# The last projection piece in two column halves, and the two transposes of a token tile side by side

## The reference

```
def layer_norm(x, g, b):
    mu = mean(x); var = mean(square(x - mu))
    return (x - mu) * rsqrt(var + LN_EPS) * g + b

x = layer_norm(DEEPNORM_ALPHA * x + h, ln_mix_g[l], ln_mix_b[l])
x = layer_norm(DEEPNORM_ALPHA * x + swiglu(x, w_gate, w_up, w_down), ln_ffn_g[l], ln_ffn_b[l])
```

## Time and profile before

| | us |
|---|---|
| median of 3 runs | 1202.56 (1202.39 to 1202.94) |
| span of the profiled execution, first to last instruction | 1201.0 |
| TensorE busy | 1191.7 |
| VectorE busy | 881.1 |
| ScalarE busy | 661.8 |
| last matmul ends | 1194.2 |
| last VectorE instruction ends | 1199.0 |

### The profile page before, as it was taken

One profiled execution on the slowest core, in us unless ns is written; L12 is line 12 of the kernel. 1 busy time (PEld: TensorE's weight loads), 2 busy tenths in 40 slices (PEclk: granted clock), 3 DMA queues, 4 the chain that ended last, 5 costly groups with the idle time before them and its releaser, 6 DMA issues.

```text
span 1201.0 us, 16544 instructions
## 1 busy us (share of the span) xinstructions
PE 1191.7 (99%) x6611; PEld 1025.8 (85%) x6611; DVE 881.1 (73%) x1227; ACT 661.8 (55%) x871; POOL 52.7 (4%) x75
## 2 busy tenths in 40 slices
PE   9999999999999999999999999999999999999997
PEld 8888888888777888888899888888889977888886
DVE  6977989847786798884688877776467667777744
ACT  6545666634566666663587645444337775544430
POOL 0000000000000000000005200000012001000000
PEclk9999999999999999999999999999999999999999
DMA  9755555564534555556434556555526433755530
GB/s 359 248 206 192 174 179 192 187 221 170 195 114 138 188 180 179 203 201 216 160 102 141 185 211 236 191 195 191 179 91 229 176 140 106 253 202 175 198 119 35
DMA packets 32652, 217.80 MB, mean 181 GB/s; under 512 B 3760, under 2 KB 4032, under 8 KB 8000
## 3 DMA queue, kind: packets, MB, share of 16 engines
q1 hardware_dynamic: 30704, 210.39, 49.5%
q0 software_dynamic: 1728, 6.29, 1.6%
q10 hardware_dynamic: 144, 0.07, 0.0%
HBM read 215.67 MB, written 1.05 MB: 180 GB/s over the span
## 4 chain that ended last, share of the span: by engine, by line
PE 99%; DVE 1%; DMA 0%; ACT 0%; issue 0%
PE ps L963 43%; PE ps L893 24%; PE ps L899 14%; PE ps L901 4%; PE ps L915 2%; PE ps L912 2%; PE ps L911 2%; PE ps L1004 1%; PE ps L977 1%; PE ps L1032 1%; PE ps L1014 1%; PE ps L1096 1%; DMA t<-in_cst 0%; PE ps L1042 0%; PE ps L1081 0%; PE ps L926 0%
## 5 line engine op out<-in xcount | busy, mean ns | idle before, releaser
L963 PE MATMUL ps<-t,t 128*128 128x512 f32 (+3 forms) x2328 | 538.4, 387 | 0.0
L1552 DVE TENSOR_TENSOR t<-t,t 128x2048 fp32r<-128x2048 f32 (+3 forms) x200 | 448.8, 2257 | 101.9 <-PE ps L963 87.7
L963 PEld LDWEIGHTS ps<-t,t 128*128 128x128 f32 x2328 | 423.1, 188 | 81.5 <-issue 1.8
L1205 ACT CAST t<-t 128x2048 fp32r<-128x2048 f32 (+3 forms) x200 | 374.6, 1883 | 202.3 <-PE ps L963 106.0
L893 PE MATMUL ps<-t,t 128*128 128x512 f32 x1274 | 305.8, 390 | 0.0
L893 PEld LDWEIGHTS ps<-t,t 128*128 128x128 f32 x1274 | 238.9, 188 | 51.2
L899 PEld LDWEIGHTS ps<-t,t 128*128 128x128 f32 x1456 | 187.2, 191 | 7.4
L899 PE MATMUL ps<-t,t 128*128 128x256 f32 x1456 | 189.5, 283 | 0.0
L1687 DVE TENSOR_REDUCE t<-ps 128x512 f32<-128x1024 f32 x40 | 49.0, 1225 | 44.3 <-PE ps L901 44.3
L1640 DVE SCALAR_TENSOR_TENSOR t<-t,t,t 128x254 f32<-128x254 f32 (+1 forms) x176 | 73.2, 478 | 10.2 <-ACT t L1230 10.2
L1270 ACT CAST t<-t 128x512 fp32r<-128x512 f32 x44 | 27.3, 620 | 91.2 <-DVE t L1671 91.2
(11 more groups left out here) (220 smaller groups left out, 846.0 us busy)
## 6 DMA issues: line engine op xcount, KB each, us to landing
t<-in_wts SPq DMA_DIRECT2D x192, 1024.0 KB, 4.9
t<-in_rows POOLq DMA_DIRECT2D x12, 512.0 KB, 4.4
t<-in_wts SPq DMA_DIRECT2D x4, 528.0 KB, 4.1
t<-in_wts SPq DMA_DIRECT2D x2, 768.0 KB, 4.8
t<-in_wts SPq DMA_DIRECT2D x2, 592.0 KB, 3.8
t<-in_x_in SPq DMA_DIRECT2D x2, 512.0 KB, 4.3
out<-t SPq DMA_DIRECT2D x4, 256.0 KB, 2.0
t<-in_wts SPq DMA_DIRECT2D x2, 256.0 KB, 6.3
```

The costliest lines, as they stand in the source:

```text
L963: ins = mm(ps[:, t_bank(stage, t, j), 0:c1 - c0], a, w[:, k, c0:c1], start=kt == 0 and part == 0, stop=kt == KTS[stage] - 1 and part == 2)
L1205: copy(wh[:, k, 0:w], wraw[:, r, 0:w]).then_inc(s_hi, 1)
L1552: tt(wl[:, k, 0:w], wraw[:, r, 0:w], wh[:, h, 0:w].bitcast(F32), ALU.subtract).then_inc(s_lo, 1)
```

## The change

At b = 8 the parts of (1,1) become "piece" steps: first all 6 k-tiles for columns 512 to 767, in the bank as before (bank 3), and then all 6 for columns 768 to 1023, in bank 4, where they start a new sum; the earlier k-tiles of these columns stay in bank 3. VectorE's `added_piece` follows each: the first makes ALPHA * x plus bank 3 for all 512 columns and the statistics of the first 256; the second adds bank 4 to the last 256 columns and makes their statistics. Tile 1's statistics are now in four records of 256 columns, tile 0's stay in two of 512.

At the inner norms the two turns of a tile stand side by side. Tile 0: behind the third of the four part steps of (1,1) at norms 1 to 4 (before: second and third), behind the fourth at norms 5 to 7 (before: third and fourth). Tile 1, in the next projection's head: behind two lo steps at norms 1 to 4 (before: none and two), behind six at norms 5 to 7 (before: four and eight).

```
--- end_steps, 5 <= b < 8
-            if n in (2, 3):
-                out.append(("turn", b, 0, n - 2))
+            if n == 3:
+                out += [("turn", b, 0, 0), ("turn", b, 0, 1)]
--- end_steps, other b
+    if b == 8:
+        for piece in range(2):
+            out += [("piece", stage, kt, piece) for kt in kts] + [("add_piece", piece)]
+        return out + [("stats", 8, 1)] + [(kind, 8, 1, j) for kind in ("centre", "norm") for j in range(2)]
-        if b < 8 and n in (1, 2):
-            out.append(("turn", b, 0, n - 1))
+        if b < 8 and n == 2:
+            out += [("turn", b, 0, 0), ("turn", b, 0, 1)]
--- head_steps
-    n = 4 if b >= 5 else 0
-    out = [("hi", stage, kt, 0) for kt in range(8)] + lo[:n] + [("turn", b, 1, 0)]
-    n, m = n, (8 if b >= 5 else 2)
-    out += lo[n:m] + [("turn", b, 1, 1)] + lo[m:]
+    n = 6 if b >= 5 else 2
+    out = [("hi", stage, kt, 0) for kt in range(8)] + lo[:n] + [("turn", b, 1, 0), ("turn", b, 1, 1)] + lo[n:]
--- t_part
+                    at = 0
+                    if piece is not None:
+                        at = 256 * piece
+                        c0, c1 = c0 + at, c0 + at + 256
+                    first, bank = kt == 0, t_bank(stage, t, j)
+                    if piece == 1:
+                        at, bank, first = 0, 4, kt == KTS[stage] - LAST[stage] * per
+                        pe.wait_ge(*ffn_read(3, 20))
+                    ins = mm(ps[:, bank, at:at + c1 - c0], a, w[:, k, c0:c1],
+                             start=first and part == 0, stop=kt == KTS[stage] - 1 and part == 2)
--- VectorE
+        def added_piece(i):
+            dve.wait_ge(s_t, T_AT["piece", "down3", KTS["down3"] - 1, i])
+            cols = slice(512, 1024) if i == 0 else slice(768, 1024)
+            if i == 0:
+                dve.own(stt(out=XN[:, 1, cols], in0=X[:, 1, cols], scalar=ALPHA, in1=acc(1, 1), op0=ALU.mult, op1=ALU.add))
+            else:
+                dve.own(tt(XN[:, 1, cols], XN[:, 1, cols], ps[:, 4, 0:256], ALU.add))
+            dve.settle()
+            dve.own(nc.vector.bn_stats(out=st[:, 44 + 6 * i:50 + 6 * i], in_=XN[:, 1, 512 + 256 * i:768 + 256 * i]))
--- VectorE, added at b = 8, t = 1 (j = 0)
+                    for i in range(2):
+                        dve.own(nc.vector.bn_stats(out=st[:, 32 + 6 * i:38 + 6 * i], in_=rs[:, 256 * i:256 * i + 256]))
--- VectorE, stats at b = 8
+            dve.own(nc.vector.bn_aggr(out=st[:, 16 * t + 12:16 * t + 14], in_=st[:, 32:56] if t else st[:, 0:12]))
```

More of the change, by code:

```diff
@@ L241, in end_steps @@
             out += [("stats", b, 0)] + normed_steps(b, 0, 0) + normed_steps(b, 0, 1)
+    if b == 8:
+        for piece in range(2):
+            out += [("piece", stage, kt, piece) for kt in kts] + [("add_piece", piece)]
+        return out + [("stats", 8, 1)] + [(kind, 8, 1, j) for kind in ("centre", "norm") for j in range(2)]
     for n, kt in enumerate(kts):
         out.append(("part", stage, 1, 1, kt))
-        if b < 8 and n in (1, 2):
-            out.append(("turn", b, 0, n - 1))
+        if b < 8 and n == 2:
+            out += [("turn", b, 0, 0), ("turn", b, 0, 1)]
     out.append(("add", b, 1, 1))
-    if b == 8:
-        return out + [("stats", b, 1)] + [(kind, b, 1, j) for kind in ("centre", "norm") for j in range(2)]
     return out + [("rest", b, 0, 0), ("stats", b, 1), ("rest", b, 0, 1), ("norm", b, 1, 0), ("norm", b, 1, 1)]
@@ L344, in releases @@
         return kt == KTS[stage] - 1 or ((t, j) == (1, 1) and kt % PER[stage] == PER[stage] - 1)
+    if s[0] == "piece":
+        _, stage, kt, piece = s
+        return kt == KTS[stage] - 1
     return False
@@ L940, in second_half, with t_part @@
             ins.then_inc(s_f, 1)
-        def t_part(step, stage, kt, t, js, passes=(0, 1, 2)):
+        def t_part(step, stage, kt, t, js, passes=(0, 1, 2), piece=None):
             per = PER[stage]
@@ L962, in t_part @@
                     c0, c1 = cols[j]
-                    ins = mm(ps[:, t_bank(stage, t, j), 0:c1 - c0], a, w[:, k, c0:c1],
-                             start=kt == 0 and part == 0, stop=kt == KTS[stage] - 1 and part == 2)
+                    at = 0
[8 more added lines that the diff above has]
+                             start=first and part == 0, stop=kt == KTS[stage] - 1 and part == 2)
             if releases(step):
@@ L1160, in pe_program @@
                 t_part(s, k[0], k[3], k[1], [k[2]])
+            elif kind == "piece":
+                t_part(s, k[0], k[1], 1, [1], piece=k[2])
             elif kind == "turn":
@@ L1577, in added @@
                 dve.wait_ge(s_add, 4 * (b - 1) + 2 * t + j + 1)
-                dve.own(nc.vector.bn_stats(out=o, in_=rs))
+                if t == 0:
+                    dve.own(nc.vector.bn_stats(out=o, in_=rs))
+                else:
+                    for i in range(2):
+                        dve.own(nc.vector.bn_stats(out=st[:, 32 + 6 * i:38 + 6 * i], in_=rs[:, 256 * i:256 * i + 256]))
                 return
@@ L1599, in stats @@
             dve.settle()
-            dve.own(nc.vector.bn_aggr(out=st[:, 16 * t + 12:16 * t + 14], in_=st[:, 16 * t:16 * t + 12]))
+            dve.own(nc.vector.bn_aggr(out=st[:, 16 * t + 12:16 * t + 14], in_=st[:, 32:56] if t else st[:, 0:12]))
             dve.settle()
@@ L1925, in dve_program @@
                 mean(*k)
+            elif kind == "add_piece":
+                added_piece(*k)
             elif kind == "stats":
```

## The result

| | before | changed |
|---|---|---|
| median, us | 1202.58 (1202.17 to 1203.29, 21 runs) | 1204.45 (1204.10 to 1204.79, 21 runs) |
| span of the profiled execution, us | 1201.0 | 1203.1 |

The ratio is 1.0015, 95% interval 1.0009 to 1.0021: slower, by 1.87 us between the medians, which is clear of zero and inside the 0.2% that the prediction puts between a difference and none. The forecast was 1204.8.

A forecast was written before the change was run, and what follows sets the result against it. Bound: TensorE's own stream plus what follows its last matmul. Waits at norms 5 to 7 (+2.76), grouping (-0.27) and tail (-0.30) sum to +2.2 us on the 1202.6 median: 1204.8, range 1202.9 to 1205.9.

The forecast's parts named there:

- the gain from grouping: Inner norms: each change between transposes and matmuls costs about 0.02 us; 14 pairs grouped give -0.27 us.
- Norms 5 to 7, tile 0: Next head's first weight load waits for ScalarE's copy of the first turn: 0.55 us per norm, bounds 0.51 to 0.57.
- Norms 5 to 7, tile 1: With only two low passes after both turns, TensorE waits for copy and subtraction: 0.37 us per norm, bounds 0.30 to 0.43.
- Norms 1 to 4: Inner norms 1 to 4: no new wait; head's first weight load is free at 1.34 us, just when due.
- The tail: After the last wide matmuls: TensorE +0.24, VectorE's way to the aggregate -0.55, aggregate +0.01; in all -0.30 us.
- The shorter price of the Trainium skill: Tail matmuls at N divided by 2.4 GHz plus about 2.5 ns: only +0.05 us for TensorE; not used.
- Dear restarts: Norms 5 to 7: nine restarts after waits at 0.11 us each, tile 1 paying 0.43 in full; +3.4 us, 1206.0, chance 0.22.
- Tile 1 covered: Norms 5 to 7: low passes and load overlap hide tile 1's chain, only tile 0 pays; +1.1 us, 1203.7, chance 0.16.
- No stall: Inner norms: the moved turns cause no waits and only the two gains are left; -0.6 us, 1202.0, chance 0.07.
- One step failed: Norm 5, tile 1: VectorE's norm halves end near 710.2 and 710.9, behind copies some 0.1 us later, making no wait.

The follow-up runs named there:

- e3: The kernel before with only tile 0's two turns of norms 5 to 7 moved behind the last group of matmuls; 1204.16 against 1202.48 us, ratio 1.0013.
- e4: The kernel before with only tile 1's two turns of norms 5 to 7 moved behind the sixth low pass; 1203.29 against 1202.48 us, ratio 1.0007.
- e10: The kernel before with tile 0's two turns of norms 1 to 4 behind the last group of matmuls; 1204.54 against 1202.48 us, ratio 1.0016.
- e1: The kernel before with the tail's change alone, all inner-norm turns where they stood; 1202.43 against 1202.48 us, ratio 0.9999.
- e6: The changed kernel with grouped turns of norms 5 to 7 earlier: tile 0 behind the third group, tile 1 behind four low passes; 1203.52 against 1202.47 us.
- e2: The kernel before with the turns grouped at norms 1 to 4 alone; 1202.49 against 1202.48 us, ratio 0.9999.
- e5: The changed kernel with the turns of norms 5 to 7 back where they stood before; 1202.07 against 1202.47 us, ratio 0.9996.

## Why the prediction was right

The mechanism and the places came out, and so did the sum (+2.2 forecast, +1.9 between the medians, +2.0 in the profile's own terms); the waits are a little smaller than I made them. The profile's figures for norms 5 to 7 have the gain from grouping in them, which the forecast had as a term of its own (0.02 us for each tile), so it is added back here.

- **Norms 5 to 7, tile 0** (0.55 taken, 0.51 to 0.57 bounds): 0.49 to 0.53 in e3, which changes nothing else, so 0.51 to 0.55. The load follows the copy by 0.06 us, at the low end of the wake-up times I had (0.05 and 0.12).
- **Norms 5 to 7, tile 1** (0.37 taken, 0.30 to 0.43): 0.29 to 0.31 in e4, which changes nothing else, so 0.31 to 0.33. The load that waits for the subtraction is 0.43 us idle, as computed, and about 0.1 of it comes back. In the changed kernel, with the matmuls' starts read one by one, the third matmul starts at 713.42, right behind its load at 713.41, where in the undisturbed stream a matmul starts a step of 0.23 behind its load; the next one then stands 0.34 behind it and not 0.23. The load that waits 0.21 us for the copy costs little: its matmul (712.76) is a plain step of 0.23 behind the one ahead of it, and the next step is 0.28, so 0.05 us. I took the middle of the bounds, and the low one was nearer.
- **Why tile 0 gets nothing back.** A load that follows transposes stands right ahead of its matmul even without a wait, so its lateness passes on in full. Before, behind the second turn of norm 5:

```profile
705.66 4.43 PEld L963 LDWEIGHTS ps<-t,t 128*128 128x128 f32 x20
705.69 4.83 PE L963 MATMUL ps<-t,t 128*128 128x512 f32 x20
```

- **Norms 1 to 4**: -0.15 us for -0.16, and no wait. The copy frees the head's first load 1.29 us after the first transpose (704.94 to 706.23 in e3) and the load is due at 1.34, so only 0.05 us is to spare. e10 shows the same wait there as soon as the cover is taken away.
- **Grouping itself**: at norms 2 to 4 it is 0.04 us or a little more for each norm, at norm 1 only 0.01. At norms 5 to 7 it isn't separable from the waits.
- **The tail** (-0.30): -0.24. TensorE's part is +0.23 (+0.24 taken) and VectorE's way to the aggregate -0.53 (-0.55 taken); the term most mis-sized is the aggregate, +0.05 for twelve more numbers where I had 0.01. The shorter price of the Trainium skill (page "TensorE: Matmul & The Clock Gate", section "Wait — 56ns, not 53.3ns?") gives as an estimate a last sum 0.05 us later; e1 measured 0.23, and this agrees with the trace's own steps.
- **The sum.** Norms 5 to 7 were forecast at +2.76 less 0.12 for their six pairs, so +2.64, and took +2.42; the tail is 0.06 short the other way. That makes 0.16 of the 0.35 us between the forecast and the median. The rest lies between the profile's own terms (+2.03) and the medians (+1.87, with an interval from 1.1 to 2.5 us) and in the forecast's rounding; no run separates it further.
- **Rivals.** Dear restarts: no. The step behind tile 1's late matmul is 0.11 us longer, the very amount that this rival took, but the matmul itself starts earlier behind its load by more than that, and behind tile 0's wait the first step is 0.31 us, as in the undisturbed stream behind transposes. Tile 1 covered: no, e4. No stall: no, e3.
- **One step failed, without weight in the sum.** I had the norm halves of tile 1 at norm 5 end some 0.1 us later than before, because the statistics stand behind the copies on ScalarE. They come earlier, at 709.12 against 709.35, which is 0.32 us along the stream. What I had left out is that VectorE's chain starts with the last group of (1,1), and that group now ends 0.45 us earlier. The copies do hold the chain up, but by 0.12 us only. L1597 (L1624 after) adds the epsilon and needs ScalarE's sum of squares; it stands behind VectorE's centring (L1629, L1656 after). Before:

```profile
706.63 1.54 DVE L1629 SCALAR_TENSOR_TENSOR t<-t,t,t 128x512 f32<-128x512 f32 x2
707.57 0.19 ACT L1221 ACTIVATION_READ_ACCUMULATOR ps<-t,t 128x1 f32 x1
708.09 0.15 DVE L1597 TENSOR_SCALAR t<-t 128x1 f32<-128x1 f32 x1
```

After:

```profile
706.28 1.54 DVE L1656 SCALAR_TENSOR_TENSOR t<-t,t,t 128x512 f32<-128x512 f32 x2
...
707.62 0.20 ACT L1234 ACTIVATION_READ_ACCUMULATOR ps<-t,t 128x1 f32 x1
707.86 0.15 DVE L1624 TENSOR_SCALAR t<-t 128x1 f32<-128x1 f32 x1
```

Before, ScalarE was done at 707.76 and the step came at 708.09, 1.46 us behind the start of the centring. After, ScalarE is done at 707.82 and the step comes 0.04 us later, 1.58 behind. That VectorE's chain starts with its matmul group is also what made me miss e6, where it starts later.

## What to carry to other kernels

A transpose, its copy and the use of it are one chain, of the same length wherever it was read here (1.3 us to the copy's user, 2.0 us to the subtraction's), and what matters is how many matmuls stand between its start and that user. Moving transposes closer to their use to save a switch to matmuls and back buys 0.02 us and can cost 0.5. And a transpose moved ahead of a matmul group delays whoever waits for that group: both sides of the group have to be counted.

## What the runs showed of the hardware

- A switch from transposes to matmuls and back costs TensorE about 0.02 us (two fewer at each of norms 2 to 4 gain 0.04; the changed kernel, e2, e5).
- A weight load in a stream of matmuls can be late at less than its own length: 0.07 us late ahead of transposes cost nothing, 0.21 ahead of a 512-column matmul cost 0.05 (changed kernel, 712.69), and that and the 0.43 behind it together cost 0.30 (e4). Behind transposes the load has no such lead: 0.49 us idle cost 0.49 to 0.53 (e3).
- A bn_stats of 256 columns takes 0.43 us, of 512 columns 0.69; two independent ones in a row 0.75 (changed kernel, 1194.30).
